# A chunked scan on one core: what tokens take from the state in one PSUM bank, the inverse by column and row halves in turns

## The reference, cut to what matters

```
def step(S, inp):
    w_t, k_t, v_t, kk_t, a_t = inp[:5]
    s_kk = jnp.einsum('nbhvk,nbhk->nbhv', S, kk_t)
    S = S * w_t[..., None, :] - s_kk[..., :, None] * (kk_t * a_t)[..., None, :] + v_t[..., :, None] * k_t[..., None, :]
    y_t = jnp.einsum('nbhvk,nbhk->nbhv', S, inp[5]) if emit else None
    return S, y_t
```

## Time and profile before

| | us |
|---|---|
| median of 3 runs | 5167.89 |
| fastest and slowest run | 5162.53, 5167.89 |
| profiled run | 5159.72 |
| its span | 5157.9 |
| TensorE busy in the span | 4904.7 |
| VectorE busy | 1477.7 |
| ScalarE busy | 1081.9 |

### The profile page before, as it was taken

One profiled execution on the slowest core, in us unless ns is written; L12 is line 12 of the kernel. 1 busy time (PEld: TensorE's weight loads), 2 busy tenths in 40 slices (PEclk: granted clock), 3 DMA queues, 4 the chain that ended last, 5 costly groups with the idle time before them and its releaser, 6 DMA issues.

```text
span 5157.9 us, 63190 instructions
## 1 busy us (share of the span) xinstructions
PE 4904.7 (95%) x27502; PEld 2724.0 (53%) x27502; DVE 1477.7 (29%) x2777; ACT 1081.9 (21%) x2070; POOL 322.0 (6%) x302
## 2 busy tenths in 40 slices
PE   8999999999999999999999988988999999989999
PEld 4444444444444445665455577877544555544444
DVE  3622110462211101000424266663301443410100
ACT  1231000122100102110322143433111333311210
POOL 1100000110000000000023000000000100000000
PEclk9999999989999999999999999998999999989999
DMA  3141212124122111111234222121211000111221
GB/s 118 72 189 66 82 64 85 51 99 162 72 75 71 67 49 57 49 49 41 95 134 143 90 76 74 54 70 51 96 52 50 27 27 14 43 41 57 90 74 57
DMA packets 91842, 378.39 MB, mean 73 GB/s; under 512 B 7984, under 2 KB 33712, under 8 KB 62128
## 3 DMA queue, kind: packets, MB, share of 16 engines
q1 hardware_dynamic: 80608, 332.92, 18.3%
q0 software_dynamic: 9808, 37.75, 2.2%
q10 hardware_dynamic: 1152, 3.67, 0.2%
HBM read 334.46 MB, written 39.85 MB: 73 GB/s over the span
## 4 chain that ended last, share of the span: by engine, by line
PE 92%; DVE 4%; ACT 2%; issue 2%; DMA 0%; POOL 0%; POOLq 0%; DVEq 0%; ACTq 0%; SPq 0%
PE ps L521 42%; PE ps L333 25%; PE ps L542 7%; PE ps L3368 2%; PE ps L1781 2%; PE ps L339 1%; PE ps L3295 1%; PE ps L990 1%; PE ps L946 1%; PE ps L3379 1%; PE ps L2478 1%; PE ps L3298 1%; PE ps L3294 1%; PE ps L3296 1%; PE ps L449 0%
## 5 line engine op out<-in xcount | busy, mean ns | idle before, releaser
L521 PE MATMUL ps<-A,W 128*128 128x512 f32 (+1 forms) x5408 | 2172.8, 562 | 24.0 <-DVE A L493 8.8
L521 PEld LDWEIGHTS ps<-A,W 128*128 128x128 f32 x5408 | 1028.0, 191 | 1117.2 <-issue 1074.3
L333 PE MATMUL ps<-A,W 64*64 64x64 f32 (+3 forms) x3264 | 708.0, 384 | 44.9 <-DVE R L2919 13.9
L333 PEld LDWEIGHTS ps<-A,W 128*128 128x128 f32 (+2 forms) x3264 | 394.5, 166 | 338.7 <-issue 306.8
L333 PE MATMUL ps<-A 64*64 64x64 f32 (+3 forms) x8416 | 493.0, 243 | 63.7 <-ACT A L3521 23.2
L333 PEld LDWEIGHTS ps<-A 64*64 64x64 f32 (+2 forms) x8416 | 451.8, 152 | 172.8 <-issue 96.7
L542 PE MATMUL ps<-W,A 128*128 128x512 f32 (+1 forms) x896 | 367.7, 572 | 1.8 <-ACT A L1567 1.8
L542 PEld LDWEIGHTS ps<-W,A 128*128 128x128 f32 x896 | 173.2, 194 | 191.8 <-issue 183.7
L435 ACT ACTIVATE A<-R 128x512 f32<-128x512 f32 (+1 forms) x96 | 52.6, 574 | 781.0 <-DVE R L1577 353.1
L1697 DVE SCALAR_TENSOR_TENSOR A<-ps,V,A 128x512 f32<-128x512 f32 (+1 forms) x48 | 31.0, 660 | 486.9 <-PE ps L333 486.3
L1577 DVE SCALAR_TENSOR_TENSOR R<-ps,MOD,R 128x512 f32<-128x512 f32 (+1 forms) x48 | 31.7, 662 | 439.3 <-PE ps L521 438.0
(11 more groups left out here) (357 smaller groups left out, 4178.0 us busy)
## 6 DMA issues: line engine op xcount, KB each, us to landing
W<-in_ada SPq DMA_DIRECT2D x48, 1024.0 KB, 5.3
W<-in_w_up SPq DMA_DIRECT2D x44, 1024.0 KB, 4.8
W<-in_w_down SPq DMA_DIRECT2D x32, 704.0 KB, 4.0
W<-in_w_in SPq DMA_DIRECT2D x18, 1024.0 KB, 4.8
W<-in_sgu_v SPq DMA_DIRECT2D x16, 1024.0 KB, 5.0
W<-in_sgu_u SPq DMA_DIRECT2D x16, 1024.0 KB, 4.8
W<-in_sgu_z SPq DMA_DIRECT2D x16, 1024.0 KB, 4.8
W<-in_sgu_o SPq DMA_DIRECT2D x16, 1024.0 KB, 4.8
```

Of the source, the lines that this page charges most:

```text
L333: r = e.matmul(out, a, b, start=start and i == 0, stop=stop and i == len(pairs) - 1, skip_group_check=loose)
L521: t = e.matmul(ps, w[:, k, c:c + mc], x(k, seg), start=k == 0, stop=k == kt - 1)
```

## The change

X goes into one bank with the first 8 heads on partitions 0 to 63 and the other 8 on 64 to 127, and its products alternate between the two column halves of the array; so does the state's part of it in H. ScalarE copies that bank in two parts of 256 columns on all 128 partitions, where it copied two banks of 512 columns on 64 partitions. The inverse Q is laid out in the same way (heads on partition halves, chunks along the columns). So it is made in one piece of 32 products over all four quarters, after P where Qa stood before it, and copied out in two copies of 128 x 512 for four of 64 x 512. U then alternates between the row halves, signals ScalarE once for both halves of the heads, and writes two banks as before. The strings of TensorE and ScalarE lose one `2`. The number of matmuls stays the same.

```
-    b.X, b.HB = A(1024), [A(8, P) for _ in range(2)]
+    b.X, b.HB = A(512), [A(8, P) for _ in range(2)]
...
 def scan_pe(pl, e):
-    scan_slots(pl, e, chosen_pe, solved_pe, carried_pe, "1 1 c 2 1 1 2 c 2 c 2 2 c 1 c c 2 2 c 2 2 2 c 2 2 2".replace(" ", ""))
+    scan_slots(pl, e, chosen_pe, solved_pe, carried_pe, "1 1 c 2 1 1 2 c 2 c 2 2 c 1 c c 2 2 c 2 2 c 2 2 2".replace(" ", ""))
...
+    def inverse():
+
+        names = [("Q", s, c) for c in range(2)]
+        ps = [take(pl, x, "0123") for x in names]
+        e.wait_ge(*S_.act_blocks.at(s, 1, "Z3"))
+        for x in names:
+            e.wait_ge(*free(pl, x))
+        for hh in range(8):
+            for g in range(2):
+                for c in range(2):
+                    t = product(e, ps[c][HALF[g], 64 * hh:64 * hh + 64],
+                                [(b.T16[HALF[c], 8 * g + hh, :], b.Z1[HALF[c], 8 * g + hh, :])])
+        t.then_inc(*S_.inverse_made.next((s, "Q")))
...
-    for g in range(2):
-        series(g, "Q", b.T16, b.Z1, S_.act_blocks.at(s, g, "Z3"))
-        yield
+    inverse()
+    yield
...
-        names = [("X", u, hf) for hf in range(2)]
-        ps = [take(pl, x, "4567") for x in names]
+        ps = take(pl, ("X", u), "4567")
...
-        for h in range(16):
-            product(e, ps[h // 8][HALF[c], 64 * (h % 8):64 * (h % 8) + 64],
-                    [(GT[HALF[c], h, :], VU[HALF[c], 64 * h:64 * h + 64])], start=h % 8 == 0, stop=False, loose=True)
+        e.wait_ge(*free(pl, ("X", u)))
+        for hh in range(8):
+            for g in range(2):
+                h = 8 * g + hh
+                product(e, ps[HALF[g], 64 * hh:64 * hh + 64], [(GT[HALF[c], h, :], VU[HALF[c], 64 * h:64 * h + 64])],
+                        start=hh == 0, stop=False, loose=True)
...
-        for p in range(8):
-            t = product(e, ps[p // 4][HALF[c], P * (p % 4):P * (p % 4) + P], [(AR[:, p, 0, HALF[c]], HB[:, p, :])],
-                        start=False, loose=True)
+        for p in range(4):
+            for g in range(2):
+                t = product(e, ps[HALF[g], P * p:P * p + P], [(AR[:, 4 * g + p, 0, HALF[c]], HB[:, 4 * g + p, :])],
+                            start=False, loose=True)
...
-        for hf in range(2):
-            e.wait_ge(*S_.state_in.at(u, "X", hf))
-            e.wait_ge(*free(pl, names[hf]))
-            if ci == 0:
-                e.wait_ge(*S_.act_blocks.at(s, hf, "Q"))
-            for h in range(8 * hf, 8 * hf + 8):
-                t = product(e, ps[hf][HALF[1 - c], 64 * (h % 8):64 * (h % 8) + 64],
-                            [(Q[HALF[c], h, :], b.X[HALF[c], 64 * h:64 * h + 64])])
-            t.then_inc(*S_.carried.next((u, "U", hf)))
+        if ci == 0:
+            e.wait_ge(*S_.act_blocks.at(s, "Q"))
+        for x in names:
+            e.wait_ge(*free(pl, x))
+        for hh in range(8):
+            if hh % 4 == 0:
+                e.wait_ge(*S_.state_in.at(u, "X", hh // 4))
+            for g in range(2):
+                t = product(e, ps[g][HALF[1 - c], 64 * hh:64 * hh + 64],
+                            [(Q[HALF[g], 8 * c + hh, :], b.X[HALF[g], 64 * hh:64 * hh + 64])])
+        t.then_inc(*S_.carried.next((u, "U")))
...
 def carried_act(pl, e, s):
...
-        for hf in range(2):
-            at = ("X", u, hf)
-            e.activation(b.X[HALF[c], 512 * hf:512 * hf + 512], bank(pl, at)[HALF[c], :], ACT.Copy).then_inc(
-                *S_.state_in.next((u, "X", hf), frees=at))
+        at = ("X", u)
+        for k in range(2):
+            cols = slice(256 * k, 256 * k + 256)
+            e.activation(b.X[:, cols], bank(pl, at)[:, cols], ACT.Copy).then_inc(
+                *S_.state_in.next((u, "X", k), frees=at) if k else S_.state_in.next((u, "X", k)))
...
-            e.wait_ge(*S_.carried.at(u, "U", hf))
+            e.wait_ge(*S_.carried.at(u, "U"))
```

More of the change, by code:

```diff
@@ L2474, in series @@
             e.wait_ge(*free(pl, x))
-        if stage != "Q":
-            for c in range(2):
-                i = one[HALF[c], :].rearrange("p (o c) -> p o c", o=1).to_broadcast([64, 8, 64])
-                e.matmul(by_heads(ps[c][HALF[c], :]), one[HALF[c], :], i, start=True, stop=False,
-                         skip_group_check=True)
+        for c in range(2):
+            i = one[HALF[c], :].rearrange("p (o c) -> p o c", o=1).to_broadcast([64, 8, 64])
+            e.matmul(by_heads(ps[c][HALF[c], :]), one[HALF[c], :], i, start=True, stop=False, skip_group_check=True)
         for hh in range(8):
@@ L2482, in series @@
                 t = product(e, ps[c][HALF[c], 64 * hh:64 * hh + 64],
-                            [(left[HALF[c], 8 * g + hh, :], right[HALF[c], 8 * g + hh, :])], start=stage == "Q",
-                            loose=True)
+                            [(left[HALF[c], 8 * g + hh, :], right[HALF[c], 8 * g + hh, :])], start=False, loose=True)
         t.then_inc(*S_.inverse_made.next((s, g, stage)))
+    def inverse():
[6 more added lines that the diff above has]
+            for g in range(2):
+                for c in range(2):
+                    t = product(e, ps[c][HALF[g], 64 * hh:64 * hh + 64],
+                                [(b.T16[HALF[c], 8 * g + hh, :], b.Z1[HALF[c], 8 * g + hh, :])])
+        t.then_inc(*S_.inverse_made.next((s, "Q")))
     def tokens(c):
@@ L2557, in carried_pe @@
             e.wait_ge(*S_.gram_masked.at(s, "G"))
-        for x in names:
-            e.wait_ge(*free(pl, x))
-        for h in range(16):
-            product(e, ps[h // 8][HALF[c], 64 * (h % 8):64 * (h % 8) + 64],
-                    [(GT[HALF[c], h, :], VU[HALF[c], 64 * h:64 * h + 64])], start=h % 8 == 0, stop=False, loose=True)
+        e.wait_ge(*free(pl, ("X", u)))
[4 more added lines that the diff above has]
+                        start=hh == 0, stop=False, loose=True)
         yield
@@ L2578, in carried_pe @@
         yield
-        names = [("U", u, hf) for hf in range(2)]
+        names = [("U", u, g) for g in range(2)]
         ps = [take(pl, x, "4567") for x in names]
-        for hf in range(2):
-            e.wait_ge(*S_.state_in.at(u, "X", hf))
-            e.wait_ge(*free(pl, names[hf]))
-            if ci == 0:
-                e.wait_ge(*S_.act_blocks.at(s, hf, "Q"))
-            for h in range(8 * hf, 8 * hf + 8):
-                t = product(e, ps[hf][HALF[1 - c], 64 * (h % 8):64 * (h % 8) + 64],
-                            [(Q[HALF[c], h, :], b.X[HALF[c], 64 * h:64 * h + 64])])
-            t.then_inc(*S_.carried.next((u, "U", hf)))
+        if ci == 0:
[9 more added lines that the diff above has]
+        t.then_inc(*S_.carried.next((u, "U")))
         yield
@@ L2615, in scan_act @@
         e.wait_ge(*event)
-    scan_slots(pl, e, chosen_act, solved_act, carried_act, "1 1 1 1 c 2 c 2 2 1 c 2 2 c 2 1 2 2".replace(" ", ""))
+    scan_slots(pl, e, chosen_act, solved_act, carried_act, "1 1 1 1 c 2 c 2 2 1 c 2 2 c 2 1 2".replace(" ", ""))
     end(pl, "scan", "act")
@@ L2653, in series @@
         e.wait_ge(*S_.inverse_made.at(s, g, stage))
-        if stage == "Q" and s >= 2:
-            e.wait_ge(*S_.carried.at(2 * (s - 2) + 1, "U", 1))
         for c in range(2):
@@ L2679, in solved_act @@
         yield
-    for g in range(2):
-        series(g, "Q", b.Q[s % 2])
-        yield
+    e.wait_ge(*S_.inverse_made.at(s, "Q"))
+    if s >= 2:
+        e.wait_ge(*S_.carried.at(2 * (s - 2) + 1, "U"))
+    for c in range(2):
+        at = ("Q", s, c)
+        e.activation(b.Q[s % 2][:, 8 * c:8 * c + 8, :], by_heads(bank(pl, at)[:, :]), ACT.Copy).then_inc(
+            *S_.act_blocks.next((s, "Q"), frees=at) if c else S_.act_blocks.next(frees=at))
+    yield
 def carried_act(pl, e, s):
@@ L2765, in chosen_dve @@
         if s and dst is b.T16:
-            e.wait_ge(*S_.inverse_made.at(s - 1, 1, "Q"))
+            e.wait_ge(*S_.inverse_made.at(s - 1, "Q"))
         for k in range(2):
```

2 lines of the change are left out of this document (1 added, 1 removed).

## The result

| | us | runs |
|---|---|---|
| before, median (lowest to highest) | 5166.84 (5162.53 to 5167.89) | 4 |
| after, median (lowest to highest) | 5097.98 (5095.28 to 5105.31) | 4 |
| after / before | 0.9862, 95% interval 0.985 to 0.9875 | |
| profiled run after; its span | 5095.65; 5093.9 | 1 |

The change takes 68.9 us off (the interval is 65 to 78), where 67 had been forecast: 5098 us for 5101.

A forecast was written before the change was run, and what follows sets the result against it. TensorE was taken to lead, with VectorE ending the second arc of each step. Ten ordinary steps at 5.4 us (54), plus 7.3 and 6.2 for the last two, make 67 off the 5167.9 median: 5101 us, range 5080 to 5133.

The forecast's parts named there:

- X, H and U overlap: TensorE's products alternating between array halves run at twice the pace: X -0.9 us, H's first part -0.87, U -0.8.
- doesn't do what it says: Rival: quarters sharing a row half (X) or column half (U) run one after another; 5135 us, chance 0.06.
- Arc A: From X of a step's first chunk to X of its second: 2.6 us less per ordinary step.
- the clock's 1.5 us a step I leave: Half-clock stretch at b0, after X, costs some 1.5 us per ordinary step; assumed to stay.
- Arc B: From the second chunk's X to the next step's first X: ends on VectorE, so wins only 2.83 us per step.
- The last two steps: End of the scan, X and H partly priced at half clock: 7.3 us less in the last but one, 6.2 in the last.
- (1): P's wait for ScalarE's copies of U: hidden except in the last step, where U to P takes 0.93 + 0.7 us.
- (2): Stage v0 takes G's bank and so waits for VectorE's mask of G: hidden by 1.1 us.
- (3): VectorE's second turn waits for all of Q, not its second half: hidden by 1.5 us.
- (4): Stage v1 waits for the copies of Q as before for those of Q's second half: the same 0.47 us.
- (5): The next X still gets the bank of Y, so its wait for VectorE's last copy stays.
- If steps are near 44, TensorE was the bound after all.: Sign set for ordinary steps of the changed kernel: near 44 us instead of the forecast 45.9 means TensorE bounds them.

The follow-up runs named there:

- e10: Changed kernel with three of SyncE's five loads (1.25 MB) delayed until stage b0 of the next step is done: 5096.07 us, ratio 0.9849.
- e1: Changed kernel with the loops of X, H's first part and U turned inside out, so no products alternate between halves: 5143.63 us, ratio 0.9958.
- e12: Changed kernel plus one idle matmul ahead of each step's first X, three in the last two steps, two before the last b1: 5093.01 us, ratio 0.9843.
- e11: Changed kernel with both the idle matmuls ahead of X and three loads delayed until stage b0 is done: 5081.33 us, ratio 0.9823.

## Why the prediction was right, and where it wasn't

**X, H and U overlap: right.** 1.15, 1.09 and about 0.93 us to the next stage were forecast from the pace of v1 and of the transposes, and are what the rows show. Pairs of column halves over the same rows (X; H over all 128) and pairs of row halves under one column half (U) both give the full factor of two. U is seen by itself in the last chunk:

```profile
3517.97 1.15 PE L333 MATMUL ps<-A 64*64 64x64 f32 x32
```

Undoing the order alone brought back 46 us. The rival "doesn't do what it says" falls with it.

**Arc A, 26 us: 27.1, with two errors that nearly cancel.** Undisturbed it is 2.5 us shorter, as forecast. The step "the clock's 1.5 us a step I leave" was wrong: of nine low stretches at b0 two were left, 10.5 us in favour of the change. The breaks in b0 and the decay products, with the low clock behind them, were in no step of the forecast and cost 8.6. That the two nearly cancel is luck. The idle time before X did grow where no break lies in v0 or v1 (the decay products wait up to 1.0 us, X up to 1.9), and yet the low clock came less often; why, no run here tells.

**Arc B, 28 us: 33.4. This term was mis-sized.** That VectorE ends it was right (X waits for line 2938; a turn less takes 1.3 us off the arc). I counted only its two waits for TensorE, 2.83 us. The trace gives 2.18 from the chain's start to the mask of G, and 1.08 instead of 0.72 from there to Y. The difference is in rows that I read too coarsely. In these rows the mask of G, the second turn, the mask of v0 and the state's sum, none of which waits, start 0.09 to 0.15 us before their forerunner's end (3212.03 + 0.69 = 3212.72, and the mask starts at 3212.63); Y's copy starts 0.03 behind its own. The mask of G and the second turn did wait before, and then began only after it. So taking these two waits away was worth the waits and 0.09 and 0.15 us; the second turn also takes 1.90 for 2.00 us, and the wait for ScalarE's scaled copies went from 0.71 to 0.60.

**The last two steps, 13.5 us: 8.5. This term was mis-sized, and the runs show why.** I priced X and H there at half the clock, as the earlier trace rows had them, and so gave each twice its saving, 2.4 us too much in all. The low clock isn't tied to those products. X of the last step and H's first part now run partly at full clock, and others in its place at half. The first rows are X with H's first part and the Y products of the last step, the third P behind its wait for the copies of U:

```profile
3500.65 2.72 PE L333 MATMUL ps<-A,W 64*64 64x64 f32 x48 [3.52 <-DVE R L2936]
3503.30 3.68 PE L333 MATMUL ps<-W,A 128*128 128x64 f32 x16
...
3509.66 3.29 PE L333 MATMUL ps<-A 128*64 128x64 f32 x64 [0.78 <-ACT A L2719]
```

The 48 records took 2.72 us (7.25 in the earlier trace rows, 2.17 at full clock), the 16 behind them 3.68 for 2.00 at full clock. Over the two steps the low clock lasts longer in the change than before (30.6 for 21.4 us). At full clock, with idle products in both, the savings are 2.5, 2.1 and 2.1 for 2.6, 2.3 and 2.3. The largest miss is the fourth arc, B of the last step but one: 25.64 to 23.89 us, -1.75 for -3.9. It has 6.8 us of low clock in the change; in e10, which has none there, it takes 20.7, and the 25.64 of before hold 1.9 us of low clock. So the work was priced well, its clock was not.

**The hidden waits.** (1) P waits for the copies of U only in the last step (in both chunks), 0.78 us, forecast 0.7. (2) v0 never waits for the mask of G in the rows above; hidden. (3) VectorE's second turn doesn't wait; it had 0.8 us in hand and not 1.5, and moving Q 1.6 us later made it the bound at once. (4) v1 waits 0.36 us, for 0.47. (5) X still waits for the copy of Y. The decay products wait for the mask of v0 in five of ten steps (4.0 us together).

**A test that was badly put.** "If steps are near 44, TensorE was the bound after all." Undisturbed steps are 43.85, and VectorE is still last before X. Half a us of mis-sized arc B and the 1.5 us of clock together moved a step as far as a change of bound would have; the wait before X decides such a question, the length of the step doesn't. The mean ordinary step is 45.1 us, for 45.9 forecast.

**What stays open.** That the breaks are a want of instructions is inferred from the packets' times and from their shortening when loads are moved; the profile doesn't say for which engine a packet is, and no kernel here changes the instruction stream alone. The short breaks in v0 and v1 (products at 15 ns a record, the closest of the scan) end at the same distance from a packet, 2.2 to 3.2 us, but no experiment was made on them.

## What to carry to other kernels

Order products so that consecutive ones fall on different quarters of the array; it cost nothing here and doubled the pace of X, H's first part and U. Then read which engine is last at the end of each arc, and price there its waits and not the work of the engine that got faster; 0.9 us in Q, for whose result VectorE waits, counted nearly in full in every step, though TensorE itself was not the last there. Price a saving at full clock and judge the low stretches apart from it, best with a few idle products in both versions: here they told some 60 us of work from some 9 of clock.

## What the runs showed of the hardware

- Four 64x64 quarters in turn bring one record each 15 ns (64 in 1.1 us), two quarters one each 30 ns (32 in 1.15 us), whichever half they share, and one quarter one each 59 ns (32 in 2.05 us); two runs on different halves overlap at their seam (H's first part 1.58 us in e1, for 1.96).
- TensorE stopped for 2.7 to 5.2 us amid a stage that waited for nothing; in all ten traces that have such a stop in b0 TensorE resumed 2.5 to 3.0 us after the start of a packet of the instruction queue that came beside 2.25 MB of loads. Moving 1.25 MB of the loads let the packet start 0.9 to 2.6 us after X for 3.3 to 5.0, and the stop lasted 0.8 to 1.0 us. All 96 stops over 0.4 us, short ones included, ended 2.2 to 3.2 us after a packet's start.
- In the change's step four VectorE instructions that wait for nothing (mask of G, second turn, mask of v0, state's sum) start 0.09 to 0.15 us before the end of the one before, so the two waits that went were worth slightly more than their length. It isn't so everywhere: Y's copy starts 0.03 us behind.
- Idle products that nobody reads, in time in which TensorE waits anyway, kept the granted clock at 1.00 through b0 in nine of ten steps of the kernel before and took 20.5 us off it. Off the changed one they took 5.7 us on one chip (e12), and 17.4 together with three loads moved (e11).
